# Compressed queries with features on partitions, their norm's token factor moved to the heads

## The reference, cut to what matters

```
u  = rmsnorm(h, ln_mix)                        # per token, over 1024 features
cq = rmsnorm(u @ w_dq, q_norm)                 # compressed query: 512 features, norm over them
q  = (cq @ w_q_b).reshape(T, 16 heads, 64 + 32)
q_nope = rmsnorm(q[..., :64], qn_nope)         # per head
q_rope = rope(rmsnorm(q[..., 64:], qn_rope), pos)
```

## Time and profile before

| | us |
|---|---|
| median of three runs | 1854.26 |
| span of the profiled execution | 1854.9 |
| TensorE busy | 1813.8 (98% of the span) |
| DVE busy | 1135.7 (61%) |
| ACT busy | 827.8 (45%) |
| GpSimd busy | 231.8 (12%) |

### The profile page before, as it was taken

One profiled execution on the slowest core, in us unless ns is written; L12 is line 12 of the kernel. 1 busy time (PEld: TensorE's weight loads), 2 busy tenths in 40 slices (PEclk: granted clock), 3 DMA queues, 4 the chain that ended last, 5 costly groups with the idle time before them and its releaser, 6 DMA issues.

```text
span 1854.9 us, 28269 instructions
## 1 busy us (share of the span) xinstructions
PE 1813.8 (98%) x10561; PEld 1734.3 (93%) x10561; DVE 1135.7 (61%) x1709; ACT 827.8 (45%) x1424; POOL 231.8 (12%) x286
## 2 busy tenths in 40 slices
PE   9999999999999999999999999999998999999997
PEld 8999999799888999999999999986777899999997
DVE  6545447879889654544874544456777755545444
ACT  5333336665565433323553333346665543333232
POOL 1000010311311000011400001132112130000110
PEclk9999999999999999999999999999999999999999
DMA  6444444456452534444444444440225434344441
GB/s 210 119 130 126 143 139 150 153 205 231 122 204 86 201 117 133 124 140 141 117 138 133 123 125 145 138 154 29 58 73 149 155 114 145 119 130 125 143 141 57
DMA packets 67652, 249.74 MB, mean 135 GB/s; under 512 B 8312, under 2 KB 9592, under 8 KB 66288
## 3 DMA queue, kind: packets, MB, share of 16 engines
q1 hardware_dynamic: 57584, 205.32, 36.4%
q0 software_dynamic: 9984, 43.27, 7.0%
HBM read 235.77 MB, written 12.12 MB: 134 GB/s over the span
## 4 chain that ended last, share of the span: by engine, by line
PE 81%; DVE 10%; ACT 3%; DMA 2%; issue 2%; POOL 1%; SPq 0%; DVEq 0%; ACTq 0%; POOLq 0%
PE pair L1899 23%; PE pair L1901 23%; PE pair L1900 23%; DVE wlo L1239 2%; PE pair L2309 2%; PE pair L2310 2%; PE pair L2311 2%; PE pair L2400 1%; DVE cy L1367 1%; DVE S L1463 1%; DMA lowA<-in_cacheT 1%; DMA wv<-in_wv 1%; DMA raw<-in_stream 1%; PE pair L1906 0%; PE pair L1908 0%
## 5 line engine op out<-in xcount | busy, mean ns | idle before, releaser
L1899 PE MATMUL pair<-xh,whi 128*128 128x384 f32 x1928 | 649.7, 337 | 3.4 <-DVE xl L1249 2.9
L1901 PE MATMUL pair<-xh,wlo 128*128 128x384 f32 x1928 | 644.5, 334 | 0.0
L1900 PE MATMUL pair<-xl,whi 128*128 128x384 f32 x1928 | 644.3, 334 | 0.0
L1239 DVE TENSOR_TENSOR wlo<-raw,whi 128x1024 fp32r<-128x1024 f32 (+3 forms) x372 | 465.6, 1253 | 176.4 <-ACT whi L702 167.2
L702 ACT ACTIVATE whi<-raw 128x1024 fp32r<-128x1024 f32 (+2 forms) x369 | 378.4, 1029 | 271.8 <-PE pair L1901 258.6
L1899 PEld LDWEIGHTS pair<-xh,whi 128*128 128x128 f32 x1928 | 361.9, 188 | 10.2 <-issue 4.6
L1900 PEld LDWEIGHTS pair<-xl,whi 128*128 128x128 f32 x1928 | 362.0, 188 | 1.6 <-issue 1.0
L1901 PEld LDWEIGHTS pair<-xh,wlo 128*128 128x128 f32 x1928 | 361.9, 188 | 0.0
L1259 DVE TENSOR_TENSOR tg<-pair,rstd 128x384 f32<-128x384 f32 x88 | 49.1, 558 | 328.0 <-PE pair L1901 327.3
L1899 PE MATMUL pair<-ah,whi 128*128 128x384 f32 x704 | 236.6, 336 | 0.0
L1901 PE MATMUL pair<-ah,wlo 128*128 128x384 f32 x704 | 236.6, 336 | 0.0
(11 more groups left out here) (401 smaller groups left out, 2249.1 us busy)
## 6 DMA issues: line engine op xcount, KB each, us to landing
raw<-in_stream SPq DMA_DIRECT2D x372, 512.0 KB, 3.6
S<-in_ssm POOLq DMA_DIRECT2D x4, 2048.0 KB, 9.4
out_ssm_s<-S POOLq DMA_DIRECT2D x4, 2048.0 KB, 7.8
seg<-acs_rows POOLq DMA_DIRECT2D x12, 512.0 KB, 5.8
cTb<-in_cacheT POOLq DMA_DIRECT2D x10, 512.0 KB, 4.2
kn<-rs_rows SPq DMA_DIRECT2D x16, 264.0 KB
lowC<-in_cache SPq DMA_DIRECT2D x8, 512.0 KB, 3.2
lowA<-in_cacheT POOLq DMA_DIRECT2D x6, 512.0 KB, 5.4
```

Of the source, the lines that this page charges most:

```text
L1239: V.tensor_tensor(wlo[:, r, 0:w], raw[:, r, 0:w], whi[:, r, 0:w].bitcast(F32), ALU.subtract).then_inc(lo_ready, 1)
L1899: M(out, whi[:, r, ws], mh_(k), start=first and k == k0, stop=False)
L1900: M(out, whi[:, r, ws], ml_(k), start=False, stop=False)
L1901: ins = M(out, wlo[:, r, ws], mh_(k), start=False, stop=last and k == k1 - 1)
```

## The change: what it does

DQ is made by `product`, so that 128 of the 512 compressed features lie on partitions and tokens along the row, one block for each of the banks 4 to 7. No transposes are needed. Each result is kept unnormalized: ACT squares it (`cqs`) and copies it times the gains to the high part (`cqh`, in the memory of `cTh`), DVE subtracts to the low part (`cql`, in `wkh`) and adds up the squares. After the first QB block TensorE sums two things per token into bank 7, the input's squares (`sqacc`) and the squares of the result (`cqs`, in `lowC`). With m the mean square of the input and c that of the unnormalized result, the two norms together divide by sqrt(c + EPS * (m + EPS)); DVE and ACT make its reciprocal in `rows[:, 0]`. It enters per token as the scale of the heads' squares and as a third operand of the evacuations. The gains come with the other gains, and one of the five small loads goes.

```
# scalar (ACT)
-            for b in range(4):
-                hi_split(DQ + b + 3)
-            token_std(5, 1)
...
-            act.wait_ge(cq_turn_ps, 1)
-            for k in range(4):
-                A(xh[:, k, :], bank[4 + k][:, 0:TOK], ACT.Copy).then_inc(cq_hi, 1)
+            for j in range(4):
+                hi_split(DQ + j + 3)
+                act.wait_ge(blk, CRED + DQ + j + 1)
+                A(cqs[:, j, :], bank[4 + j][:, 0:TOK], ACT.Square)
+                A(cqh[:, j, :], bank[4 + j][:, 0:TOK], ACT.Copy, scale=gains[:, NORMS + 1, j:j + 1]).then_inc(cq_hi, 1)
...
-                A(sq5[:, e % 2, 0:384], bank[3 * (cg % 2) + t][:, 0:384], ACT.Square).then_inc(q_sq, 1)
+                A(sq5[:, e % 2, 0:384], bank[3 * (cg % 2) + t][:, 0:384], ACT.Square,
+                  scale=rows[:, 0, t:t + 1]).then_inc(q_sq, 1)
...
+                    if cg == 0 and b == 0:
+                        act.wait_ge(cq_ms, 1)
+                        A(rows[:, 0, :], rows[:, 1, :], ACT.Sqrt).then_inc(cq_std, 1)
+                        act.wait_ge(cqn_ready, 1)
# vector (DVE)
+            for j in range(4):
+                lo_split(DQ + j + 3)
+                dve.wait_ge(cq_hi, j + 1)
+                V.scalar_tensor_tensor(out=cql[:, j, :], in0=bank[4 + j][:, 0:TOK], scalar=gains[:, NORMS + 1, j:j + 1],
+                                       in1=cqh[:, j, :].bitcast(F32), op0=ALU.mult, op1=ALU.subtract).then_inc(cq_lo, 1)
+                if j:
+                    ins = V.tensor_tensor(cqs[:, 0, :], cqs[:, 0, :], cqs[:, j, :], ALU.add)
...
+            dve.wait_ge(w_ld, 16 * 4)
...
+                    if cg == 0 and b == 0:
+                        dve.wait_ge(rt_ps, 2)
+                        step(V.tensor_scalar(rows[:, 1, :], bank[7][:, 0:TT], EPS / D_MODEL, EPS * EPS, ALU.mult, ALU.add))
+                        V.scalar_tensor_tensor(out=rows[:, 1, :], in0=bank[7][:, TT:2 * TT], scalar=1.0 / Q_LORA,
+                                               in1=rows[:, 1, :], op0=ALU.mult, op1=ALU.add).then_inc(cq_ms, 1)
+                        dve.wait_ge(cq_std, 1)
+                        V.reciprocal(rows[:, 0, :], rows[:, 0, :]).then_inc(cqn_ready, 1)
+                        dve.wait_ge(cqn_ready, 1)
...
-                    V.tensor_tensor(q[:, :, 0:NOPE], src[:, :, 0:NOPE], bc(sm[:, o + 16:o + 20], (P, 4, NOPE), 2),
-                                    ALU.mult).then_inc(qb_evac, 1)
+                    V.scalar_tensor_tensor(out=q[:, :, 0:NOPE], in0=src[:, :, 0:NOPE], scalar=rows[:, 0, t:t + 1],
+                                           in1=bc(sm[:, o + 16:o + 20], (P, 4, NOPE), 2), op0=ALU.mult,
+                                           op1=ALU.mult).then_inc(qb_evac, 1)
# tensor (TensorE)
+            pe.wait_ge(cT_ready, 1)
+            for j in range(4):
+                weights(DQ + j)
+                for k in range(KD):
+                    if j == 0:
+                        pe.wait_ge(xl_ready, 40 + k + 1)
+                    ins = product(bank[4 + j][:, 0:TOK], (DQ + j) % SLOTS, k, k + 1, *X, k == 0, k == KD - 1)
+                ins.then_inc(blk, 1)
+
+            def compressed_rows():
+                pe.wait_ge(cq_ready, 1)
+                token_rows(5, bank[7])
+                for t in range(TT):
+                    ins = M(bank[7][:, TT + t:TT + t + 1], cqs[:, 0, tiles(t)], ones[:, 0:1], start=True, stop=True)
+                ins.then_inc(rt_ps, 1)
...
+                    if b == 0 and cg == 0:
+                        compressed_rows()
```

More of the change, by code:

```diff
@@ L104, in build @@
         wlo = sb("wlo", [P, SLOTS, 1024], F32R)
-        gains = sb("gains", [P, NORMS + 1, KD])
+        gains = sb("gains", [P, NORMS + 2, KD])
         ident = sb("ident", [P, P])
@@ L234, in build @@
         vnew = ckv[:, 0:2, :]
-        cqr = lowC[:, 0:TT * Q_LORA].rearrange("p (t c) -> p t c", t=TT)
-        qgr = Pb[:, 0, 0:Q_LORA]
+        cqs = lowC[:, 0:4 * TOK].rearrange("p (j t) -> p j t", j=4)
+        cqh = cTh[:, :, :, :].rearrange("p a k t -> p (a k t)")[:, 0:4 * TOK].rearrange("p (j t) -> p j t", j=4)
+        cql = wkh[:, :, :].rearrange("p k c -> p (k c)")[:, 0:4 * TOK].rearrange("p (j t) -> p j t", j=4)
         mk = ckv[:, 0:2, :].rearrange("p a c -> p (a c)")[:, 0:TOK]
@@ L352, in build @@
         cqn_ready = sem("cqn_ready")
-        cq_turn_ps = sem("cq_turn_ps")
+        cq_ms = sem("cq_ms")
         cq_hi = sem("cq_hi")
@@ L1654, in _ @@
             down(2, 5)
[L1657 to L1666, removed]
+            for j in range(4):
[5 more added lines that the diff above has]
+                    ins = V.tensor_tensor(cqs[:, 0, :], cqs[:, 0, :], cqs[:, j, :], ALU.add)
+                    if j < 3:
+                        step(ins)
+                    else:
+                        ins.then_inc(cq_ready, 1)
+            dve.wait_ge(w_ld, 16 * 4)
             V.tensor_tensor(gq[:, 2:3], gq[:, 0:1], gq[:, 1:2], ALU.mult).then_inc(gq_ready, 1)
@@ L2170, in _, with token_rows @@
             ple_pe(0, 3)
-            def token_rows(m):
+            def token_rows(m, out):
                 pe.wait_ge(sq_done, m + 1)
                 for t in range(TT):
-                    ins = M(bank[4][:, t:t + 1], sqacc[:, m % 2, tiles(t)], ones[:, 0:1], start=True, stop=True)
-                ins.then_inc(rt_ps, 1)
+                    ins = M(out[:, t:t + 1], sqacc[:, m % 2, tiles(t)], ones[:, 0:1], start=True, stop=True)
+                return ins
             pe.wait_ge(pin_ready, 8)
@@ L2200, in _ @@
             down(2, 5)
-            for b in range(4):
-                weights(DQ + b)
-                pe.wait_ge(xl_ready, 40 + 2 * b + 2)
-                for t in range(TT):
[L2207 to L2221, removed]
+            pe.wait_ge(cT_ready, 1)
[9 more added lines that the diff above has]
+                token_rows(5, bank[7])
+                for t in range(TT):
+                    ins = M(bank[7][:, TT + t:TT + t + 1], cqs[:, 0, tiles(t)], ones[:, 0:1], start=True, stop=True)
+                ins.then_inc(rt_ps, 1)
             def q_transpose(e):
@@ L2240, in _ @@
                         for t in range(TT):
-                            ins = row_product(bank[3 * (cg % 2) + t][:, 0:384], n % SLOTS, 384 * kk, 384, xh[:, k, tiles(t)],
-                                              xl[:, k, tiles(t)], k == 0, k == 3)
+                            ins = row_product(bank[3 * (cg % 2) + t][:, 0:384], n % SLOTS, 384 * kk, 384, cqh[:, k, tiles(t)],
+                                              cql[:, k, tiles(t)], k == 0, k == 3)
                     ins.then_inc(blk, 1)
-                    if b == 0 and cg >= 2:
+                    if b == 0 and cg == 0:
+                        compressed_rows()
+                    elif b == 0 and cg >= 2:
                         q_transpose(3 * cg - 4)
@@ L2513 @@
     put("kv", row_blocks(A["w_kv_a"], 3))
-    put("dq", row_blocks(A["b_w_dq"][0], 2))
+    put("dq", tile_blocks(A["b_w_dq"][0]))
     for cg in range(4):
@@ L2555 @@
     arr["sin"] = np.tile(np.sin(ang_).astype(f32), 2).reshape(TT, P, -1).transpose(1, 0, 2)
-    arr["qgr"] = every(A["b_q_norm"][0])
     arr["gr"] = every(A["b_qn_rope"][0])
```

23 lines of the change are left out of this document (6 added, 17 removed).

## The result

The changed kernel takes 1857.99 us (median; 1855.83 to 1860.72), the kernel before beside it on the same chip 1855.01 (1851.14 to 1857.82): a ratio of 1.0019, 95% interval [1.0013, 1.0025]. So it is 2.4 to 4.6 us slower, where 4.3 us faster was forecast, and it lies outside the range. No rival gave this either: the only slower one needed a late load, and that load was in time.

What follows compares the result with a forecast made beforehand. TensorE stands still between DQ and QB, awaiting the wv load and the normalization chain. Gaining 4.68 us there, less 0.2 and 0.22 for the heads, gives 4.26 off 1854.26: 1850.0 us, eight-in-ten range 1849.0 to 1852.6.

Steps and rivals of the forecast that it cites:

- the sum: Whole kernel: 4.68 - 0.2 - 0.22 = 4.26 us gained, taken off the median 1854.26, giving 1850.0.
- The terms of the stage: TensorE's compressed-query stage: DQ 16.64 us, first QB block 3.12, six one-column sums 1.34.
- The matmul behind 36 products: TensorE after two QB blocks: the next matmul, before at 1232.59, comes 4.68 us earlier.
- The covers: Four things to hide beside TensorE: feature tiles for DQ, sums of squares, token factor, splits of the QB weights.
- The sum of squares: ACT and DVE behind DQ: complete about 1222.9, wanted at 1223.45, margin 0.5 us.
- The table load: ACT, token factor: runs from about 1223.9 to 1225.2, beside DVE's low split, ended before the mean square is there.
- The rival with the late load: DVE's wait for wv, heads queued behind it: landing at 1232.3 gives 1857.6 us; chance 0.03.
- What the heads pay: Head squares on ACT 0.085 us longer, two DVE evacuations 0.067 each: rows reach GpSimd 0.22 us later.
- The stall at the transposes: TensorE at the transposes starting at 1246.41, waiting for GpSimd's rows: 0.2 us of stall.
- The wait on GpSimd behind QB: TensorE after the last QB product: already 0.4 us, whole 0.22 paid on top, about 0.6.
- The port rival: Head evacuations reading an SBUF column lock GpSimd out of the shared port: gain 1.7 us, time 1852.5; chance 0.14.
- Swallowed behind the stage?: Later past-key loads might absorb up to the whole gain, 1854.3 us; chance 0.13, shared with the gap being kept.

Runs made afterwards that it cites:

- the addresses restored: Changed kernel with the small tile `rows` moved behind the attention's tiles, so all moved tiles lie at their old addresses: 1850.24 us against 1855.53, ratio 0.9975.

## Why the prediction was wrong, point by point

**The step that failed** is the one sentence of the sum: "what lies around the stage is the same in both". The working looked at instructions and queues, not at addresses. The diff shows the wider `gains`; I priced its load (one of five goes) and not its 32 bytes. What the runs show in its place: the step in the four down projections went from 0.1733 to 0.1767 us, 7.0 us that the sum put at nothing. With the addresses restored, and the rest of the change in place, the measured gain is 2.6 to 6.5 us around 4.6, and the forecast had 4.26. That 1850.24 stands so close to the forecast's 1850.0 is partly luck: the kernel before took 1855.53 beside it, not the 1854.26 that the forecast started from. And that the old addresses give the short step is nothing that the working had looked at.

**The terms of the stage**, all read off the changed kernel. DQ: 16.64 worked out, 1208.93 to 1225.58 = 16.65 measured. First QB block: 3.12, measured 3.12 (1225.58 to 1228.70). Six column sums: 1.34, measured 1.26 to the start of the next product (1228.70 to 1229.96), and 1.34 with the long first step behind them (0.259 us instead of 0.173), which the forecast's 0.67 for three had in it. The matmul behind 36 products: 4.68 earlier, measured 4.61. The rest was lost to QB's own step, which the sum took at 0.1733 and which was 0.1767 in the second block. With the addresses restored QB runs at 0.1767 from its first block on (18 products in 3.18 us, 1220.60 to 1223.78), and in five of the other seven; by the starts in the trace that is 0.35 us over the eight blocks.

**The covers.** Rows of ACT and DVE in order of time in the changed kernel, and the load of `wv` (the last number is from issue to landing):

```profile
1228.82 1.28 ACT L1011 ACT_TABLE_LOAD   x1
...
1239.78 0.58 ACT L991 ACTIVATE sq<-pair,rows 128x384 f32<-128x384 f32 x1 [2.87 <-PE pair L1913]
```

```profile
1227.31 0.55 DVE L1659 TENSOR_TENSOR lowC<-lowC 128x384 f32<-128x384 f32 x1
1227.77 0.15 DVE L1666 TENSOR_TENSOR gq<-gq 128x1 f32<-128x1 f32 x1
...
1230.33 0.16 DVE L1684 SCALAR_TENSOR_TENSOR rows<-pair,rows 128x3 f32<-128x3 f32 x1
...
1245.03 0.35 DVE L1704 SCALAR_TENSOR_TENSOR kn<-pair,rows,sm 128x128 f32<-128x128 f32 x1
1245.30 0.47 DVE L1706 SCALAR_TENSOR_TENSOR kn<-pair,rows,sm 128x256 f32<-128x256 f32 x1
```

```profile
wv<-in_wv POOLq DMA_DIRECT2D x1, 1024.0 KB, 9.5
```

The sum of squares is complete at 1227.86, 0.84 before TensorE asks for it at 1228.70 (0.5 worked out). The table load, 1.28 as in the earlier trace rows, ends at 1230.10, before the mean square is there at 1230.49. The product of gains at 1227.77 follows at once, so the wait for `wv` costs nothing: issued at 1214.2, landed after 9.5 us at 1223.7. The rival with the late load has no footing.

**What the heads pay.** The evacuations take 0.35 and 0.47 (0.36 and 0.48 worked out), the scaled square 0.58 (0.57). The stall at the transposes: the row of 1247.14 takes 1.26 where the undisturbed ones take 1.03, so 0.23 for 0.20. (The forecast's own rows made it 0.12: 0.22 later than 1246.75, wanted at 1246.85. It took 0.2 without saying why, and that came out.) The wait on GpSimd behind QB went from 0.4 to 0.5, not to 0.6. From the start of DQ to the first product with `wk` it is 48.93 us (1208.93 to 1257.86); before, it was 53.12, since that product starts at 1256.81:

```profile
1256.81 1.02 PE L2257 MATMUL pair<-wk,cT 128*128 128x512 f32 x2
```

The net gain of the stage is 4.19 for 4.26, and 4.01 with the addresses restored (49.11 us).

**The port rival** fell. GpSimd's long operation is still there, and still beside DVE's low split:

```profile
1245.40 0.33 POOL L617 TENSOR_TENSOR kn<-kn 128x64 f32<-128x64 f32 x1
...
1248.81 1.02 POOL L617 TENSOR_TENSOR kn<-kn 128x64 f32<-128x64 f32 x1
```

```profile
1248.69 0.96 DVE L1235 TENSOR_TENSOR wlo<-raw,whi 128x768 fp32r<-128x768 f32 x1
```

Both GpSimd rows are the same operation of the rotation. The first lies wholly beside the evacuation of 1245.30, with its column from SBUF, and takes 0.33, where undisturbed ones take 0.32. The second lies beside the low split, which reads two tensors of SBUF, and takes 1.02. The Trainium skill ("SBUF — State Buffer", "SBUF: two separate sides") has the lock taken by a DVE operation with two SBUF inputs; the trace agrees for the two tensors of the split (1.02), and adds that the column doesn't count as an input (0.33).

**Swallowed behind the stage?** Not the whole of it. With the addresses restored the lead over the profile of before is 3.8 us at the first product with `wk` and 2.8 at the span's end (1852.1 to 1854.9), and the timed runs give 2.6 to 6.5. What comes and goes in between is of that size: some executions have a stretch at the granted clock of 0.50, which is 1.2 GHz, between 1400 and 1420 us and some have none. Here is the changed kernel without it, and the restored one with it, after TensorE was busy for 2.90 of the 5 us from 1400 to 1405 at 1.00 (the kernel before has it too, 0.50 in the same two microseconds).

```profile
1400.00:1420.00 20.00, 15.29 (x124) 14.14 (x122) 18.58 (x40) 12.81 (x33) 3.01 (x5) 1.00 0.67 184
```

```profile
1410.00:1412.00 2.00, 2.00 (x11) 2.00 (x10) 1.53 (x4) 1.48 (x4) 0.00 (x0) 0.50 0.90 280
```

So one profile's span can't settle a microsecond here. The ratio's interval excludes that the whole gain is swallowed; whether a part of it is stays open.

## What to carry to other kernels

A change of a tile's size is a change to every tile allocated behind it. Before a sum over one stage is taken as the kernel's time, list which streamed tiles move, and by how many bytes, and after the run compare the step of matmuls in stages that the diff doesn't touch: 455 for 464 matmuls in 80 busy microseconds at the full clock gave the answer here. New small tiles go to the end of the allocation, or into space freed by others, so that the large operands stay where they are; and when a kernel gets slower for no reason, one run with the old addresses is cheap. That old addresses are good ones is not given, though: here some offsets gave the short step and some a longer one, and no rule was found that tells them beforehand.

## What the runs showed that was not expected

The step of a 384-column product, busy without a gap at the granted clock of 1.00, depends on where the streamed tile lies against the weights. Moves of `ah` and `al` by less than 256 bytes (the 64 together with all tiles behind `gains`, the others alone or, for 32, both ways), mean step in us where it is longer, and in which of the four down projections it is:

| move, bytes | 0 | 32 | 64 | 96 | 128 | 160 | 192 | 224 |
|---|---|---|---|---|---|---|---|---|
| longer step | | 0.1767 | 0.1760 | 0.1767 | 0.1767 | | | |
| in which | none | all | all | 1, 2, 4 | 3 | none | none | none |

All others have 0.1733 (0.1734 at 160). The longer step is not a fixed price for each product but a rhythm. The steps in ns, twelve in a row, by the starts in the trace (first down projection, for 128 bytes the third):

```
before    173 173 174 173 173 174 173 173 174 173 173 174
32 bytes  178 174 180 175 177 174 180 175 178 174 180 175
64 bytes  176 173 174 175 182 176 173 174 175 182 176 173
96 bytes  174 179 175 179 174 179 174 179 175 179 174 179
128 bytes 178 176 177 176 177 176 178 176 177 176 177 176
```

The order of the operands repeats every three products; these repeat, to within 1 ns, every four, five, two and two. So it isn't a matter of which operand comes up.

The addresses alone don't decide, and one kernel shows it. In the changed kernel the second and the sixth QB block use the same rows of the same streamed and still tiles, the same slot of the weights and the same banks. The second runs at 0.1766 behind its first step, with the steps of the 96 bytes (174 179 175 179), the sixth at 0.1733. The second (1229.96 to 1233.22, 3.26 us) begins behind the column sums, the sixth behind transposes, and ends at 1247.14 after 3.20:

```profile
1243.94 0.42 PE L1911 MATMUL pair<-whi,cTh 128*128 128x384 f32 x1
```

The third down projection, which differs from the others at 96 and 128 bytes, also begins otherwise. It stands behind the transposes of `ckv` and `krow`, where the other three follow the gate and up products at once. In all 18 profiles its second product starts 0.256 to 0.264 us after its first, in the others 0.169 to 0.181 us. The first and the third for 128 bytes:

```profile
195.51 0.33 PE L1901 MATMUL pair<-ah,whi 128*128 128x384 f32 x1
195.68 0.34 PE L1902 MATMUL pair<-al,whi 128*128 128x384 f32 x1
...
1111.39 0.27 PE L2200 MATMUL pair<-ident,krow 128*96 128x128 f32 x1
1111.42 0.42 PE L1901 MATMUL pair<-ah,whi 128*128 128x384 f32 x1
1111.68 0.34 PE L1902 MATMUL pair<-al,whi 128*128 128x384 f32 x1
```

So how a run of products begins may choose between the rhythms that an offset allows. That is argued, not shown: no run changed a beginning alone. What is left open besides: what meets what at these distances (TensorE and its weight loads are both busy for all 80 us of the rows above, but no run separated them), and why gate and up are not slow at a distance of 160.
